# Four bare pick rows in one VectorE instruction, gated by ScalarE and GpSimd, with four pick buffers

## What is computed

```python
def peer_ffn(h, w_query, keys1, keys2, expert_u, expert_v):
    ...
    top_s, top_pos = lax.top_k(cand_s, PEER_TOPK)
    idx = jnp.take_along_axis(cand_i, top_pos, axis=-1)
    gate = jax.nn.softmax(top_s.astype(jnp.float32), axis=-1).astype(h.dtype)
    ...
        act = jax.nn.gelu(jnp.einsum('thkd,td->thk', expert_u[ib], hb), approximate=False)
        return jnp.einsum('thk,thkd->td', gb * act, expert_v[ib])
```

## Time and profile before

| | |
|---|---|
| median of 3 runs | 2194.0 us (2191.49 to 2195.93) |
| profiled execution | 2195.41 us, its span in the trace 2193.4 us |
| busy share of the span | PE 94%, DVE 67%, ACT 49%, POOL 3% |
| POOL instructions | 36, 55.4 us |
| mean granted TensorE clock | 0.977 of 2.4 GHz |

### The profile page before, as it was taken

The page is one execution under the profiler, slowest core; times in us unless marked ns, Lnnn a source line. Parts: engine busy times, 40 slices in busy tenths (PEclk is TensorE's granted clock), DMA queues, the critical chain, the costliest instruction groups (busy, mean ns, idle before and its releaser), DMA issues.

```text
span 2193.4 us, 42453 instructions
## 1 busy us (share of the span) xinstructions
PE 2059.9 (94%) x15492; PEld 1953.6 (89%) x15492; DVE 1476.1 (67%) x2393; ACT 1079.0 (49%) x1659; POOL 55.4 (3%) x36
## 2 busy tenths in 40 slices
PE   7899967899999999999998999799999999999997
PEld 7898865689999999999998999689999999889997
DVE  5687699966666666666666556676556556856555
ACT  5445326944444444444445444544445444555443
POOL 0000240000000000000000000000000000000000
PEclk9899998999999999999999999999999999999999
DMA  5344430045555555555555555335555565335552
GB/s 195 120 135 146 152 116 1 0 156 187 184 191 185 187 183 191 189 184 184 189 188 168 186 174 170 125 106 188 186 174 171 181 185 180 126 125 173 183 187 100
DMA packets 95683, 348.19 MB, mean 159 GB/s; under 512 B 10752, under 2 KB 10880, under 8 KB 95360
## 3 DMA queue, kind: packets, MB, share of 16 engines
q1 hardware_dynamic: 95184, 344.88, 48.3%
q10 hardware_dynamic: 432, 2.36, 0.3%
HBM read 346.15 MB, written 1.05 MB: 158 GB/s over the span
## 4 chain that ended last, share of the span: by engine, by line
PE 81%; DVE 12%; ACT 4%; issue 2%; DVEq 0%; DMA 0%; ACTq 0%; SPq 0%
PE front L1619 39%; PE acc L1619 29%; PE tile L1619 12%; DVE w_lo L939 2%; DVE pick L1392 2%; ACT w_hi L559 2%; DVE pick L1386 1%; DVE rstd L962 1%; DVE h_lo L969 1%; DVE chosen L1368 0%; DVE x L1450 0%; DVE rest L1283 0%; DVE top_i L1279 0%; DVE top_i L1297 0%; DVE top_v L1275 0%
## 5 line engine op out<-in xcount | busy, mean ns | idle before, releaser
L939 DVE TENSOR_TENSOR w_lo<-raw,w_hi 128x1024 fp32r<-128x1024 f32 x636 | 778.2, 1224 | 188.4 <-ACT w_hi L559 188.1
L559 ACT CAST w_hi<-raw 128x1024 fp32r<-128x1024 f32 x652 | 680.5, 1044 | 360.1 <-PE front L1619 144.4
L1619 PE MATMUL front<-h_hi,w_hi 128*128 128x256 f32 x2432 | 690.2, 284 | 8.2 <-DVE h_lo L969 7.5
L1619 PE MATMUL front<-h_hi,w_lo 128*128 128x256 f32 x2432 | 689.0, 283 | 0.0
L1619 PE MATMUL front<-h_lo,w_hi 128*128 128x256 f32 x2432 | 688.9, 283 | 0.0
L1619 PEld LDWEIGHTS front<-h_hi,w_hi 128*128 128x128 f32 x2432 | 466.9, 192 | 15.1 <-DVE h_lo L969 5.4
L1619 PEld LDWEIGHTS front<-h_lo,w_hi 128*128 128x128 f32 x2432 | 467.0, 192 | 5.0
L1619 PEld LDWEIGHTS front<-h_hi,w_lo 128*128 128x128 f32 x2432 | 467.0, 192 | 0.0
L608 ACT ACTIVATE scaled<-scaled 128x256 f32<-128x256 f32 x216 | 90.2, 418 | 500.6 <-DVE scaled L1024 289.0
L1019 DVE TENSOR_TENSOR scaled<-front,rstd 128x512 f32<-128x512 f32 x88 | 60.8, 691 | 275.9 <-PE front L1619 275.8
L1619 PE MATMUL tile<-h_hi,w_hi 128*128 128x256 f32 x736 | 219.8, 299 | 23.0 <-DVE h_lo L1082 4.9
(11 more groups left out here) (254 smaller groups left out, 2622.0 us busy)
## 6 DMA issues: line engine op xcount, KB each, us to landing
raw<-stream SPq DMA_DIRECT2D x652, 512.0 KB, 3.5
x<-x_t SPq DMA_DIRECT2D x2, 512.0 KB, 4.8
keysT<-keys_t ACTq DMA_DIRECT2D x1, 1024.0 KB, 5.5
attc<-attention_constants ACTq DMA_DIRECT2D x1, 1024.0 KB, 5.6
out_t<-h SPq DMA_DIRECT2D x4, 256.0 KB, 2.2
mixc<-mixer_constants SPq DMA_DIRECT2D x1, 704.0 KB, 9.2
wpool<-w_pool ACTq DMA_DIRECT2D x1, 256.0 KB, 7.0
lane<-lanes SPq DMA_DIRECT2D x1, 128.0 KB, 4.8
```

Source lines behind the costliest of these rows:

```text
L559: nc.scalar.copy(w_hi[:, s, :], raw[:, s, :]).then_inc(hi_ready, 1)
L939: nc.vector.tensor_tensor(w_lo[:, s, :], raw[:, s, :], w_hi[:, s, :].bitcast(F32), ALU.subtract).then_inc(lo_ready, 1)
L1619: return nc.tensor.matmul(out, lhsT, rhs, start=start, stop=stop, **kw)
```

## The change

VectorE writes all four first-key matrices of a step bare in one instruction of 512 columns, and the four of second keys in another of the same form. ScalarE gates the first two, GpSimd the last two. There are four buffers for both kinds: two where `pick1` and `pick2` were (`picks_mid`), two in the first two slots of the stream ring (`picks_raw`). So VectorE waits until slabs 76 and 77 are split before it writes the third step, and SP loads slabs 80 to 83 only when all products of the stage are done (`pick_used` at 256). TensorE waits for ScalarE's count at the first two tokens of a step and for GpSimd's at the last two. Semaphore `gated_by_pool` is new and `pick1_ready` is gone.

```diff
-        pick1 = sb("pick1", MID, [4, 2, P])
-        pick2 = sb("pick2", MID + 8 * P, [2, 4, P])
+        picks_mid = sb("picks_mid", MID, [2, 2, 4, P])
+        picks_raw = sb("picks_raw", RAW, [2, 2, 4, P])
...
+        def pick_rows(b, side):
+
+            return (picks_mid if b < 2 else picks_raw)[:, b % 2, side, :, :]
+
@@ SP @@
-            at = RING
+            with sp.Fori(1, first["peer"] // RING + 1) as turn:
+                for s in range(RING):
+                    sp.wait_ge(lo_ready, turn * RING + (s + 1 - RING))
+                    sp.dma_start(raw[:, s, :], stream[bass.ds(turn * RING + s, 1), :, :]
+                                 .rearrange("a p n -> (a p) n")).then_inc(landed[s], 16)
+            sp.wait_ge(pick_used, T)
+            at = first["peer"] + RING
@@ GpSimd @@
+                    pool.wait_ge(picks_copied, 3)
+                    for turn in range(T // 4):
+                        pool.wait_ge(masks_ready, turn + 1)
+                        for c in (2, 3):
+                            to = pick_rows(turn % 4, 0)[:, c, :]
+                            nc.gpsimd.tensor_scalar(to, to, gate_T[:, 4 * turn + c:4 * turn + c + 1], None,
+                                                    ALU.mult).then_inc(gated_by_pool, 1)
@@ ScalarE @@
-                def gate_rows(t, half):
-
-                    for slot in range(4 * half + 1, 4 * half + 4):
-                        to = pick1[:, slot // 2, slot % 2, :]
-                        nc.scalar.activation(to, to, ACT.Copy, scale=gate_T[:, t(slot - 4 * half)])\
-                            .then_inc(gated_ready, 1)
+                def gate_rows(t, b):
+
+                    for c in range(2):
+                        to = pick_rows(b, 0)[:, c, :]
+                        nc.scalar.activation(to, to, ACT.Copy, scale=gate_T[:, t(c)]).then_inc(gated_ready, 1)
...
-                for half in range(2):
-                    act.wait_ge(masks_ready, half + 1)
-                    gate_rows(lambda k: slice(4 * half + k, 4 * half + k + 1), half)
+                for b in range(3):
+                    act.wait_ge(masks_ready, b + 1)
+                    gate_rows(lambda c: slice(4 * b + c, 4 * b + c + 1), b)
                 with act.Fori(0, T // 16 - 1) as turn:
                     for b in range(4):
-                        act.wait_ge(masks_ready, turn * 4 + (b + 3))
-                        gate_rows(lambda k: bass.ds(turn * 16 + (8 + 4 * b + k), 1), b % 2)
+                        act.wait_ge(masks_ready, turn * 4 + (b + 4))
+                        gate_rows(lambda c: bass.ds(turn * 16 + (12 + 4 * b + c), 1), (b + 3) % 4)
                         act.wait_ge(pick_used, turn * 16 + (4 * b + 4))
                         copy_G(bass.ds(turn * 16 + 4 * b, 4), b)
@@ VectorE @@
-                def gated_rows(t, half):
-                    ...
-                def second_rows(t, half):
-                    ...
+                def rows(t, b):
+
+                    for side, idx_T, ready in ((0, idx1_T, masks_ready), (1, idx2_T, pick2_ready)):
+                        nc.vector.tensor_tensor(pick_rows(b, side), iota.unsqueeze(1).broadcast_to([P, 4, P]),
+                                                idx_T[:, t].unsqueeze(2).broadcast_to([P, 4, P]),
+                                                ALU.is_equal).then_inc(ready, 1)
+
+                for b in range(4):
+                    if b == 2:
+                        dve.wait_ge(lo_ready, first["peer"] + 2)
+                    rows(slice(4 * b, 4 * b + 4), b)
+                with dve.Fori(0, T // 16 - 1) as turn:
+                    for b in range(4):
+                        dve.wait_ge(pick_used, turn * 16 + (4 * b + 4))
+                        rows(bass.ds(turn * 16 + (16 + 4 * b), 4), b)
@@ TensorE @@
-                    mm(o, pick1[:, 2 * (b % 2) + k // 2, k % 2, :], pick2[:, b % 2, k, :], True, True).then_inc(pick_used, 1)
+                    mm(o, pick_rows(b, 0)[:, k, :], pick_rows(b, 1)[:, k, :], True, True).then_inc(pick_used, 1)
...
+                def token_weights(b, gated, rows_):
+
+                    for c in range(4):
+                        if c < 2:
+                            pe.wait_ge(gated_ready, gated + (c + 1))
+                        else:
+                            pe.wait_ge(gated_by_pool, gated + (c - 1))
+                        if c == 0:
+                            pe.wait_ge(pick2_ready, rows_)
+                        weights(b, c, c)
+
+                for b in range(4):
+                    token_weights(b, 2 * b, b + 1)
+                with pe.Fori(1, T // 16) as turn:
                     for b in range(4):
-                        pe.wait_ge(g_copied, turn * 4 + (b + 1))
-                        ...
+                        pe.wait_ge(g_copied, turn * 4 + (b - 3))
+                        token_weights(b, turn * 8 + 2 * b, turn * 4 + (b + 1))
```

More of the change, by code:

```diff
@@ L389, in build @@
         picks_copied = sem("picks_copied")
-        pick1_ready = sem("pick_rows_with_gates_ready")
         masks_ready = sem("pick_rows_of_first_keys_ready")
         gated_ready = sem("pick_rows_gated_by_act")
+        gated_by_pool = sem("pick_rows_gated_by_pool")
         pick2_ready = sem("pick_rows_of_second_keys_ready")
@@ L744, in _ @@
                     t = T - 16 + 4 * b
-                    if b < 2:
-                        act.wait_ge(masks_ready, T // 4 - 1 + b)
-                        gate_rows(lambda k: slice(t + 8 + k, t + 9 + k), b % 2)
+                    if b == 0:
+                        act.wait_ge(masks_ready, T // 4)
+                        gate_rows(lambda c: slice(T - 4 + c, T - 3 + c), 3)
                     act.wait_ge(pick_used, t + 4)
@@ L1900, in weights @@
                         o = tile[:, 2 * b - 4 + c // 2, (c % 2) * P:(c % 2 + 1) * P]
-                    mm(o, pick1[:, 2 * (b % 2) + k // 2, k % 2, :], pick2[:, b % 2, k, :], True, True).then_inc(pick_used, 1)
+                    mm(o, pick_rows(b, 0)[:, k, :], pick_rows(b, 1)[:, k, :], True, True).then_inc(pick_used, 1)
                 pe.wait_ge(picks_copied, 3)
[L1904 to L1911, removed]
-                    for b in range(4):
-                        pe.wait_ge(g_copied, turn * 4 + (b + 1))
[L1914 to L1920, removed]
+                def token_weights(b, gated, rows_):
[10 more added lines that the diff above has]
+                with pe.Fori(1, T // 16) as turn:
+                    for b in range(4):
+                        pe.wait_ge(g_copied, turn * 4 + (b - 3))
+                        token_weights(b, turn * 8 + 2 * b, turn * 4 + (b + 1))
                 pe.wait_ge(g_copied, T // 4)
```

## The result

| | before | after |
|---|---|---|
| median | 2194.7 us (4 runs) | 2228.0 us (4 runs, 2226.6 to 2228.4) |
| profiled execution, its span | 2195.41, 2193.4 us | 2228.42, 2226.6 us |
| first row instruction to first expert matmul | 344.62 to 437.16: 92.5 us | 343.89 to 466.34: 122.5 us |

The ratio is 1.0153, 95% interval 1.0135 to 1.0170: 33 us slower where 13 were forecast. The side was right and the size was not: 2207 was too low by 21.

A forecast was written before the change was run, and what follows sets the result against it. VectorE and ScalarE, each pacing the other, were taken to bound the weight-table stage at 1.395 us a step. Forecast step 1.20 + 2 x 0.21 = 1.62; 64 steps +14.4, minus 1 for the start: +13.4, 2207 us, range 2180 to 2230.

The forecast's parts named there:

- (a): VectorE's row writing: two 512-column instructions of 0.60 us each, so 1.20 us a step instead of 1.395.
- case without contention: Weight-table stage: GpSimd's gates cost VectorE nothing, 1.20 us a step is the beat, -13.5 us, 2180.5; chance 0.15.
- The rival on the other side: Weight-table stage: one-input GpSimd gates slip in beside VectorE's rows without costly contention, 2180.5 us; chance 0.15.
- (b): ScalarE gates two rows instead of three: 1.10 us a step instead of 1.40, no longer a bound.
- (e): SP's queue: slabs 80 to 83 load after the stage, hidden behind TensorE's work; priced at nothing, 3 us at worst.
- (d): Four buffers instead of two remove VectorE's 0.06 us wait a step and 1.05 us starting stall; 1 us credited.
- (f): GpSimd gates beside VectorE's rows: each takes 0.21 us out of VectorE's time, making a step 1.62 us, +14.4 us.
- the hold is short: Weight-table stage: a gate holds VectorE 0.11 us, a step is 1.42, about 2195, no measurable change; hold under 0.14: chance 0.15.
- GpSimd becomes the bound: Weight-table stage: gates near 1.04 us, GpSimd needs 2.08 us a step, 2237 us; chance 0.10 shared with half clock.
- TensorE's half clock: Weight-table stage: TensorE granted 1.2 GHz, 1.80 us a step, 2219 us; chance 0.10 shared with GpSimd as bound.
- The estimate of 0.107 us: GpSimd gate: 128 columns at line rate and 1.2 GHz take 0.107 us, supporting a short hold on VectorE.
- the likeliest case: Weight-table stage: contention with a hold of 0.14 to 0.36 us a gate, 2207 us, range 2198 to 2227; chance 0.60.

## Why the prediction was wrong in size

- **VectorE's part (a) held.** Two instructions of 0.60, 1.20 us a step, and the stage would have run at that: with iota in PSUM it does, at 2181.9, where the forecast's case without contention stood at 2180.5. The rival on the other side was priced right; what it needed was another operand.
- **ScalarE's part (b) held.** It stopped being a bound: it is busy 26 of 40 us. Its price was 0.05 us too high, by the waiting in the 1.40.
- **Late loads (e) held, and buffers (d) as far as can be seen.** The expert layer's 728.8 us didn't change. The old split with four buffers shortens its stage by 3.3 us in the profile, but its ratio of 0.9992 doesn't prove a gain in the time.
- **Part (f) failed, the price of GpSimd.** That the engines block each other was right, and so was where. What failed is the sentence that a step is 1.20 + 2 x 0.21, with VectorE as the bound. The hold on VectorE is 0.095 us a gate, not 0.21. By that alone the step would be 1.39, the case "the hold is short". But I priced only what a gate takes from VectorE, and not what it takes on GpSimd: 0.58 us alone, of which the columns are half, and 1.30 beside rows, the time of two whole row instructions. GpSimd at 1.875 a step is the bound. The rival "GpSimd becomes the bound" had the mechanism in general, with 2.08 a step and 2237 us, from a gate as long as the 128x512 square. It got a chance of 1 in 10 with TensorE's half clock. The estimate of 0.107 us for a gate's columns isn't borne out either: the 127 columns between a one-column gate and a full one are 0.32 us, alone.
- **The range held the result by luck.** 2228 lies under 2230 only because 3 us of late loads, which cost nothing, were added to the likeliest case's end. The range was said to leave out the case with GpSimd as the bound, and that is the case which came.
- **The profile answered the prediction's own signs.** "GpSimd's gates back to back with VectorE waiting for used rows" was named as a sign of being wrong, and that is what the timeline shows. The other reading that was offered, the hold as half of what a step is over 1.20, would have misled: (1.875 - 1.20)/2 = 0.34, inside the range of 0.14 to 0.36, where the hold is 0.095. Such a reading is good only while VectorE is full.
- **Where I could have seen it.** Rows 6 show the delay on both sides: VectorE's 0.82 and 1.25 and GpSimd's 1.22 for 1.04. I turned the first into a price and used the second only as proof that both wait. VectorE's row instructions start 0.60 us apart with records of 0.68, so the other engine finds hardly a gap between them; that this is why GpSimd waits most is my reading, no run varies the gap. And a proportion to the columns of a long instruction gave 0.21 for the hold, where one of 128x128 has 0.095 and one of 128x1 none that shows. A gate's own length isn't in proportion either: 0.28 at one column and 0.60 at 128.
- **The point at which it decides** was named as a hold of 0.0975. Measured 0.095, the constant gates, with both engines at 0.695, come out at 2192.1 against 2194.0, no change: the break-even was right for a case which the real gate, with its second read, isn't.

What is shown is that the contention needs VectorE's second SBUF input, and that the gate column makes a full gate last two row instructions instead of one. What stays open: why a gate of one column, which reads the same gate column, lasts only one. Both reads of the short gate may fit into one gap of VectorE's; nothing here shows the reads themselves.

## What to carry to other kernels

Before work is handed to an idle GpSimd, look at what VectorE runs there: if its instructions have two SBUF inputs and follow each other closely, a short GpSimd instruction can last as long as one or two whole ones of them, as here, and its length is theirs, not its own. Price both directions of a contention, what the new work takes from the old and how long the new work itself becomes. If the offload is wanted, try one of VectorE's inputs in PSUM: here that turned 1.5% slower into 0.5% faster.

## What the runs showed that I had not expected

- A GpSimd multiply of 128x128 by a column takes 0.60 us alone and 1.31 beside VectorE's compare with two SBUF inputs; the same compare with one of them in PSUM leaves it at 0.604 to 0.607.
- By a constant it takes 0.53 alone and 0.72 beside: having the gate column as an operand costs 0.07 us in one case and 0.59 in the other.
- VectorE's 128x512 compare is 0.68 us with iota in SBUF and 0.68 with iota in PSUM, with no gate beside it in the first case and with gates in the second.
- With 1 instead of 128 columns a gate beside rows still takes 0.71 to 0.79 us, against 0.28 alone.
